# Decay levels of a gated linear recurrence: only the second-half columns of each chunk are multiplied, and the eight prompt chunks of a level share one PSUM bank and one copy

## The reference, cut to what matters

```python
def rec_chunk(S0, q, k, v, g):
    b = jnp.cumsum(g, axis=1)
    causal = jnp.tril(jnp.ones((C, C), dtype=bool))
    diff = jnp.minimum(b[:, :, None] - b[:, None, :], 0.0)
    decay = jnp.where(causal[None, :, :, None, None], jnp.exp(diff), 0.0)
    scores = jnp.einsum('bthk,bshk,btshk->bhts', q, k, decay)
    o = jnp.einsum('bhts,bshv->bthv', scores, v) + jnp.einsum('bthk,bhkv->bthv', q * jnp.exp(b), S0)
    b_last = b[:, -1]
    S = jnp.exp(b_last)[..., None] * S0 + jnp.einsum('bshk,bshv->bhkv', k * jnp.exp(b_last[:, None] - b), v)
    return o, S
```

## Time and profile before

| | |
|---|---|
| median of 3 runs | 1411.13 us (1408.55 to 1412.16) |
| the profiled execution | 1410.09 us, of which its span is 1408.3 us |
| PE busy | 1359.2 us, 97% of the span |
| DVE busy | 949.3 us, 67% |
| ACT, POOL busy | 649.1 us (46%), 681.1 us (48%) |
| granted clock of PE | 0.9 or more of full speed in each of 40 slices |

### The profile page before, as it was taken

One profiled execution on the slowest core, in us unless ns is written; L12 is line 12 of the kernel. 1 busy time (PEld: TensorE's weight loads), 2 busy tenths in 40 slices (PEclk: granted clock), 3 DMA queues, 4 the chain that ended last, 5 costly groups with the idle time before them and its releaser, 6 DMA issues.

```text
span 1408.3 us, 21360 instructions
## 1 busy us (share of the span) xinstructions
PE 1359.2 (97%) x8092; PEld 1206.9 (86%) x8092; DVE 949.3 (67%) x1666; ACT 649.1 (46%) x1153; POOL 681.1 (48%) x469
## 2 busy tenths in 40 slices
PE   7999999999988999999999999999999999999997
PEld 6988889999986555558879999999999999999786
DVE  5357777999995877534568585858576767677433
ACT  6355554778774655541125443443434343434111
POOL 2444445554645767740025474646565655544100
PEclk9999999999999999999999999999999999999999
DMA  8211101132213310002231111111111111107322
GB/s 259 72 31 30 31 18 44 46 93 79 82 52 121 105 29 6 30 1 90 91 95 47 31 36 46 37 46 37 46 37 46 37 46 35 48 7 213 109 90 68
DMA packets 101589, 86.81 MB, mean 62 GB/s; under 512 B 6481, under 2 KB 90321, under 8 KB 101489
## 3 DMA queue, kind: packets, MB, share of 16 engines
q1 hardware_dynamic: 99856, 80.63, 18.9%
q0 software_dynamic: 1632, 4.82, 0.9%
HBM read 65.46 MB, written 19.97 MB: 61 GB/s over the span
## 4 chain that ended last, share of the span: by engine, by line
PE 68%; DVE 19%; issue 5%; ACT 4%; POOL 3%; DMA 1%; SPq 0%; POOLq 0%; DVEq 0%; ACTq 0%
PE bank L190 29%; PE wide L1625 7%; PE bank L1522 7%; DVE marks L860 6%; PE bank L238 6%; PE bank L1066 4%; PE wide L1037 4%; PE bank L1050 2%; DVE score L925 2%; PE bank L689 2%; DVE bits L876 2%; PE wide L450 1%; PE wide L1632 1%; DVE states L1946 1%; PE wide L1635 1%
## 5 line engine op out<-in xcount | busy, mean ns | idle before, releaser
L190 PE MATMUL bank<-hn_hi,rw_hi 128*128 128x352 f32 x768 | 251.5, 327 | 1.6 <-DVE hn_lo L180 1.6
L190 PE MATMUL bank<-hn_hi,rw_lo 128*128 128x352 f32 x768 | 247.6, 322 | 0.0
L190 PE MATMUL bank<-hn_lo,rw_hi 128*128 128x352 f32 x768 | 247.4, 322 | 0.0
L190 PE MATMUL bank<-hn_hi,w_hi 128*128 128x352 f32 x648 | 211.6, 327 | 4.6 <-ACT relu L732 3.3
L190 PE MATMUL bank<-hn_hi,w_lo 128*128 128x352 f32 x648 | 208.4, 322 | 0.0
L190 PE MATMUL bank<-hn_lo,w_hi 128*128 128x352 f32 x648 | 208.2, 321 | 0.0
L1017 POOL TENSOR_SCALAR probs<-probs,low 128x128 f32<-128x128 f32 (+8 forms) x72 | 130.2, 1811 | 59.5 <-DVE low L1157 59.2
L190 PEld LDWEIGHTS bank<-hn_hi,rw_hi 128*128 128x128 f32 x768 | 144.9, 189 | 3.5 <-issue 3.0
L190 PEld LDWEIGHTS bank<-hn_lo,rw_hi 128*128 128x128 f32 x768 | 145.3, 189 | 0.0
L190 PEld LDWEIGHTS bank<-hn_hi,rw_lo 128*128 128x128 f32 x768 | 144.9, 189 | 0.0
L788 POOL TENSOR_TENSOR swapped<-swapped,sin 128x352 f32<-128x352 f32 x57 | 56.1, 984 | 167.5 <-ACT swapped L728 108.4
(11 more groups left out here) (256 smaller groups left out, 3059.7 us busy)
## 6 DMA issues: line engine op xcount, KB each, us to landing
rw_raw<-in_rec_w_in SPq DMA_DIRECT2D x32, 512.0 KB, 4.1
w_raw<-in_att_w_in SPq DMA_DIRECT2D x27, 512.0 KB, 3.9
q_rotated<-relu SPq DMA_DIRECT2D x24, 176.0 KB, 1.9
xin<-in_x_prompt SPq DMA_DIRECT2D x8, 512.0 KB, 4.2
wo_raw<-in_att_w_out SPq DMA_DIRECT2D x4, 1024.0 KB, 8.5
x_again<-in_x_prompt SPq DMA_DIRECT2D x8, 512.0 KB, 4.1
residual<-h_rows SPq DMA_DIRECT2D x8, 512.0 KB, 2.9
wf_raw<-in_rec_w_out SPq DMA_DIRECT2D x4, 1024.0 KB, 9.5
```

Of the source, the lines that this page charges most:

```text
L190: last = pe.matmul(out, l, r, start=n == 0, stop=n == len(passes) - 1)
```

## The change

The prompt becomes one group for levels 0 to 5: a new group `PROMPT` (3) covers all eight chunks, and level 6, the transposes, the states and `out` keep the groups 0, 1 and 2. At levels 0 to 5 the moving operand is cut to the second halves of the blocks, 64 columns of a chunk (16 of the sample), read with a step; the results lie packed, 8 chunks x 64 columns in one bank. The weights stay the whole chunk of 128 columns (32 for the sample). DVE reads a level of the prompt in one `copy_predicated` of 512 columns, packed on the side of PSUM and in blocks of m on the side of `pairs`. `out` of group 0 and of group 1 now both wait for the copy of level 5 of the whole prompt.

```diff
-        return (0, 1, 2) if P >> level <= DEC else (0, 1)
+        return (0, 1, 2) if level == LEVELS else (PROMPT, 2) if P >> level <= DEC else (PROMPT,)
...
     def group(g):
+        if g == PROMPT:
+            return slice(0, SEQ), slice(0, SAMPLE), P
...
-                    out = wide[0:r, i % 4, j * P:(j + 1) * P]
+                    out = wide[0:r, i % 4, j % 4 * P:(j % 4 + 1) * P]
...
-                        left, right = (k[:, slot, at_c], q[:, slot, at_c]) if level == LEVELS else (
-                            levels[:, level, at_c], levels[:, level, at_c])
-                        last = pe.matmul(out[:, 0:r], left, right, start=True, stop=True)
+                        if level == LEVELS:
+                            last = pe.matmul(out[:, 0:r], k[:, slot, at_c], q[:, slot, at_c], start=True, stop=True)
+                        else:
+                            out = wide[0:r, i % 4, j * (P // 2):j * (P // 2) + r // 2]
+                            last = pe.matmul(out.rearrange("p (n m) -> p n m", m=P >> (level + 1)), levels[:, level, at_c],
+                                             seconds(levels[:, level, at_c], level)[:, :, 1, :], start=True, stop=True)
...
-                            pe.wait_ge(dve_read, n_dve[at["pairs", head, g, LEVELS - 1] + 1])
+                            pe.wait_ge(dve_read, n_dve[at["pairs", head, 2 if g == 2 else PROMPT, LEVELS - 1] + 1])
...
-                before = {g: at["pairs", head, g, LEVELS] for g in range(3)}
+                before = {PROMPT: at["pairs", head, 1, LEVELS], 2: at["pairs", head, 2, LEVELS]}
...
-                        part = wide[0:r, i % 4, :].rearrange("p (c x) -> p c x", x=P)[:, 0:n, 0:r]
-                        part = seconds(part, level)[:, :, :, 1, :]
+                        part = wide[0:r, i % 4, 0:n * r // 2].rearrange("p (c n m) -> p c n m", c=n, m=m)
```

More of the change, by code:

```diff
@@ L1388, in recurrence @@
     PER_HEAD = 12
+    PROMPT = 3
     products, at = [], {}
```

## The result

The changed kernel takes 1423.99 us (median of 4 runs, 1423.65 to 1433.44) against 1410.25 us of the kernel before (median of 4). Over all these runs the ratio is 1.0108, with a 95% interval of 1.0089 to 1.0127; the medians alone give 1.0097. It is slower, as forecast, but by 13.7 us where 8 were forecast, and the time lies outside the range of 1412 to 1422. The profiled execution is the slowest of the four, 1433.44 us with a span of 1431.7 us.

The account below looks back on a forecast made before the run. PE was taken to bound the kernel, its level records paced by weight loads. Wait 1.21 less gain 0.2 gave 1.0 us a head, 8 us for 8 heads: 1418 profiled, 1419 us forecast, range 1412 to 1422.

Parts of the forecast that it names:

- The pace of the records: PE, levels 0 to 5: weight load keeps records at 0.112 us despite 64 columns, gain 0; bounds 0.056 and 0.112.
- these durations are at the upper clock: PE's levels, `out` and projections in the kernel before: PEclk 1.00 in all three stretches, taken as 2.4 GHz.
- The new wait: PE before `out`: all of it waits for level 5's single copy, 1.59 us where it was 0.38, cost 1.21 a head.
- The sample's gaps: PE around the sample's product: shorter last streams shrink the gaps at levels 2, 3 and 4, gain 0.2 us a head.
- the array running empty: PE, weights going from 128 columns to 32: load 0.20 us after the last record, not 0.11; half stream takes 0.05 off.
- the right bound: DVE's level-5 copy of 512 columns: bounds 0.69 and 1.26 us; 1.26 taken, with the mask as what costs.
- The fast copy: Rival, level 5's last copy: PSUM side was slow, copy now takes 0.69 us; 1414.6 us in all, chance 0.30.
- The fast stream: Rival, PE levels 0 to 5: streaming sets the pace, records of 0.056 us; 1376 us in all, chance 0.08.
- Stepped reading slowing the stream: Rival, PE at level 5, perhaps 4: short runs make 64 columns take 0.21 us; 1432 us, chance 0.05.
- The chances given for slower: Whole kernel slower by over 0.3%: forecast 0.50, stepped reading 0.05, a third of the full-speed copy's 0.30, stated as 0.66.

Follow-up runs that it names:

- The filled stream: Changed kernel with seven of eight prompt chunks per level streaming their second halves twice, 128 columns, the wait in front of `out` kept: 1420.54 us, ratio 1.0074.
- the kernel without the wait: Changed kernel with the prompt of levels 0 to 5 in two groups again, still 64 moving columns: 1410.67 us, median of ten runs, ratio 1.0025.
- The two experiments: Changed kernel with the masks stored packed, 1424.44 us; changed kernel with level 5's prompt copy writing its 512 columns in a row of `pairs`, 1417.32 us.
- the kernel with one bank: Kernel before with the sample's four level products of a head as one product in one bank, behind the prompt's level 5: 1404.08 us, ratio 0.9952.

## Why the prediction was wrong, point by point

- **The pace of the records** was right. 0.112 us with 64 columns, and 0.058 as soon as the weights shrink too. The Trainium skill's figure for a load ("TensorE: Matmul & The Clock Gate", section "LDWEIGHTS (loading the stationary operand)") is borne out at both widths: 107 and 53 ns against 112 and 58 between records.
- **The step that failed is the one that isn't there: the granted clock.** The words "these durations are at the upper clock" were read from the kernel before and carried over to a kernel that streams half of the time; no rival had another clock. The clock costs about 5 us by the medians (13.7 less 8.6) and 15 in the profiled execution; without it the sum is 1419, as forecast. The filled stream shows whose it is: same wait, same loads, double the columns, and no fall in any head. It too lies 2 us above its sum, by a fall outside the recurrence, so the half streams' own part is 1.6 to 3.5 us by the medians (1422.12 and 1423.99 less 1420.54).
- **The new wait** was right in place and a little short: 1.21 us forecast, 1.36 measured. Measured from the last prompt record (1036.90, which is 1036.56 and three records of 0.112) to `out` (1038.64) it is 1.74, less 0.38: 1.36 us. The copy started 0.31 us after the record, not 0.26 (the shorter stream didn't bring the result forward), and took 1.29 instead of 1.26. PE's record came 0.14 after its end; the forecast's 0.07 led to the weight load and not to the record, and the load came 0.11 after it (1038.61). A reading in the same step was off without changing it: at level 4 the sample's copy starts 0.34 us after the group's, not about 0.27.
- **The sample's gaps** were forecast at a gain of 0.2 us a head and gave 0.26 (12.18 to 11.92 in the kernel without the wait), but not in the way described. The gap that was put down to the array running empty stayed at 0.20 us (1036.90 to the load of 1037.10), so it doesn't hang on the length of the last stream. What shrank is behind the small product: at level 5 the second full record comes 0.16 us after the first (1035.17 to 1035.34), where it was 0.21 (1021.98 to 1022.20). The sum of wait and gain, 1.36 - 0.26, is the 1.1 us of the levels. That it is so near the forecast's 1.0 is in part luck: the wait was 0.15 too short and the gain 0.06.
- **Why level 5's copy is slow.** The forecast took the right bound for a wrong reason. The argument ruled out `pairs` because `tensor_tensor` writes the same blocks at full speed, and left mask and PSUM. The two experiments rule out the mask and show `pairs`. The row that was used was one of another instruction, and the 1.26 us came out right by luck. The rule of "Vector Engine (DVE) Microarchitecture Reference", section 5.2, in the Trainium skill, that runs of two adjacent words keep a port at full rate, holds for the `tensor_tensor` rows here (690 ns for 528 columns) and not for the destination of `copy_predicated` (1.29 us for 512).
- **The rivals.** The fast copy fell, with 1.29 us. The fast stream fell, with the pace. Stepped reading slowing the stream fell: level 5's records stayed 0.112 us apart. The direction was right and the range, 1412 to 1422, had no room for the clock. The chances given for slower, 0.50, 0.05 and a third of 0.30, add up to 0.65 and not 0.66.

## What to carry to other kernels

Before halving the streamed columns of a matmul, look at what sets the pace of its records: two first loads after a wait show the load's length, and here the load of full fp32 weights (0.112 us) was already as long as the stream of 128 columns. Then columns taken away buy nothing, and they may cost the granted clock, so a change of PE's duty needs a case with another clock in its range. Merging two reads into one takes away their overlap with the next stage, and small products with other weights gained 6.7 us when they went into one bank, behind one another, and nothing in banks of their own.

## What the runs showed of the hardware that was not expected

- The granted clock fell to its lower level while PE had no gap: 0.56 over 19.85 us of records 0.112 us (at full clock) apart with 64 streamed columns (two groups, no wait). It was 1.00 in all heads of the profiles with 128 streamed columns or with 64 columns of weights beside 64 streamed.
- `copy_predicated` with 512 columns takes 1.29 us when it writes fp32 blocks of 2 columns and 0.71 us with blocks of 4; packing its mask or its source changes nothing, packing its destination gives 0.72.
- After weights of 128 columns PE starts weights of 32 columns 0.20 us after the last record, with 64 streamed columns as with 128; between small products of like weights it is about 0.03 us a record (in the kernel with one bank).
